# An expert layer's output side: gathering pv row by row, or streaming all of pv against a table of weights

## The reference

```python
def peer(h, w_pq, pk1, pk2, pu, pv):
    q = (h @ w_pq).reshape(n, P_HEADS, 2, P_HALF)
    s1 = jnp.einsum('nhd,hkd->nhk', q[:, :, 0], pk1)      # 128 keys each
    s2 = jnp.einsum('nhd,hkd->nhk', q[:, :, 1], pk2)
    v1, i1 = lax.top_k(s1, P_TOPK)                        # 16 best
    v2, i2 = lax.top_k(s2, P_TOPK)
    cand = (v1[..., :, None] + v2[..., None, :]).reshape(n, P_HEADS, P_TOPK * P_TOPK)
    cidx = (i1[..., :, None] * P_NKEYS + i2[..., None, :]).reshape(...)
    sc, j = lax.top_k(cand, P_TOPK)
    e = jnp.take_along_axis(cidx, j, axis=-1)             # 128 experts of 16384
    g = jax.nn.softmax(sc, axis=-1)
    a = jax.nn.gelu(jnp.einsum('nhkd,nd->nhk', pu[e], h), approximate=False)
    return jnp.einsum('nhk,nhkd->nd', g * a, pv[e])
h2 = layer_norm(DN_ALPHA * h1 + peer(h1, ...), ln2_g, ln2_b)
```

## Time and profile before

| what | us |
|---|---|
| runs (3) | 4841.81, 4850.69, 4885.9; median 4850.69 |
| span of the profiled execution | 4854.9 |
| busy PE, DVE, POOL, ACT | 3808.4, 2587.8, 2443.7, 821.8 |
| gathers L1351 and L1357, 1056 each | busy 1179.8 and 1225.1 |
| moved by the gathers' queue | 1107.96 MB |

### The profile page before, as it was taken

The page is one execution under the profiler, slowest core; times in us unless marked ns, Lnnn a source line. Parts: engine busy times, 40 slices in busy tenths (PEclk is TensorE's granted clock), DMA queues, the critical chain, the costliest instruction groups (busy, mean ns, idle before and its releaser), DMA issues.

```text
span 4854.9 us, 35025 instructions
## 1 busy us (share of the span) xinstructions
PE 3808.4 (78%) x10196; PEld 1735.7 (36%) x10196; DVE 2587.8 (53%) x5932; ACT 821.8 (17%) x1886; POOL 2443.7 (50%) x2256
## 2 busy tenths in 40 slices
PE   9899898878999667888676667677778667667677
PEld 4444445545664523333222222223234222222222
DVE  0323239997214675666565465465556656445453
ACT  1210123332100111111111111111111111111111
POOL 0000000000000077777777777777777777777776
PEclk9889989987799889999999999999999999999999
DMA  2100100000210499999999999999999999999998
GB/s 82 36 2 2 55 19 20 14 7 1 70 35 27 128 340 347 354 333 332 355 364 363 366 367 360 367 372 362 362 364 388 352 355 355 359 359 353 352 368 320
DMA packets 405562, 1185.00 MB, mean 244 GB/s; under 512 B 39936, under 2 KB 125248, under 8 KB 405264
## 3 DMA queue, kind: packets, MB, share of 16 engines
q0 software_dynamic: 304384, 1107.96, 61.2%
q1 hardware_dynamic: 101008, 74.99, 5.1%
HBM read 1176.60 MB, written 6.20 MB: 244 GB/s over the span
## 4 chain that ended last, share of the span: by engine, by line
POOL 20%; DMA 17%; PE 15%; issue 9%; DVE 5%; ACT 1%; POOLq 0%; DVEq 0%; SPq 0%; ACTq 0%
DMA v_rows<-in_pv,v_rows_at 14%; PE acc L1412 11%; POOL u_rows L1351 10%; POOL v_rows L1357 9%; PE pq_ps L1379 4%; DMA u_rows<-in_pu,u_rows_at 2%; DVE u_rows L1614 1%; PE key_ps L1387 0%; DVE key_at L1507 0%; DVE one_hot L1600 0%; ACT diag L1461 0%; DVE one_hot L1596 0%; DVE key_top L1504 0%; DVE top_at L1507 0%; DVE expert_f L1602 0%
## 5 line engine op out<-in xcount | busy, mean ns | idle before, releaser
L1412 PE MATMUL acc<-v_rows,diag 128*128 128x512 f32 (+1 forms) x4224 | 2064.5, 623 | 840.6 <-DMA v_rows<-in_pv,v_rows_at 587.5
L1614 DVE CUSTOM_DVE_ANT_0 u_rows<-u_rows,late 128x1024 f32<-128x1024 f32 x1056 | 1274.2, 1226 | 1061.5 <-DMA u_rows<-in_pu,u_rows_at 1054.7
L1412 PEld LDWEIGHTS acc<-v_rows,diag 128*128 128x128 f32 (+1 forms) x4224 | 751.2, 192 | 2135.1 <-issue 1261.4
L1357 POOL DMA_INDIRECT v_rows<-in_pv,v_rows_at x1056 | 1225.1, 1160 | 325.3 <-issue 235.8
L1351 POOL DMA_INDIRECT u_rows<-in_pu,u_rows_at x1056 | 1179.8, 1117 | 369.9 <-issue 291.3
L1461 ACT ACTIVATE diag<-ident_sb,expert_w 128x128 f32<-128x128 f32 x1024 | 379.7, 397 | 1451.4 <-PE acc L1412 1364.6
L1338 POOL COPY u_rows_at<-expert 128x16 uint32<-128x16 uint32 (+1 forms) x66 | 20.2, 306 | 1193.2 <-DVE expert L1605 1180.8
L1379 PE MATMUL pq_ps<-xT_sb,w_pq_sb 128*128 128x256 f32 (+2 forms) x768 | 238.8, 465 | 8.2 <-DMA iota_sb<-in_iota 7.6
L306 POOL DMA_DIRECT2D out_gla_p<-gla_S x4 | 2.3, 587 | 480.9 <-DVE gla_S L630 480.9
L1504 DVE MAX8 key_top<-key_scores 128x8 f32<-128x128 f32 (+1 forms) x288 | 68.1, 283 | 271.2 <-ACT key_scores L1447 171.3
L930 DVE MAX8 m<-score 128x8 f32<-128x384 f32 (+6 forms) x209 | 183.4, 878 | 5.3
(11 more groups left out here) (207 smaller groups left out, 3045.9 us busy)
## 6 DMA issues: line engine op xcount, KB each, us to landing
w_pq_sb<-in_w_pq SPq DMA_DIRECT2D x48, 512.0 KB, 12.6
u_rows<-in_pu,u_rows_at POOLq DMA_INDIRECT x1056, 6.2
v_rows<-in_pv,v_rows_at POOLq DMA_INDIRECT x1056, 6.2
xT_sb<-in_xT SPq DMA_DIRECT2D x8, 528.0 KB, 7.0
w_gvr<-in_w_in SPq DMA_DIRECT2D x2, 2048.0 KB, 13.0
w_gk<-in_w_in SPq DMA_DIRECT2D x8, 512.0 KB, 6.1
w_dsa<-in_w_in SPq DMA_DIRECT2D x2, 2048.0 KB, 10.3
w_b<-in_w_in SPq DMA_DIRECT2D x8, 512.0 KB, 4.2
```

The lines of the kernel that those rows point to most:

```text
L1357: pool.indirect_dma_start(out=V[:, j % RING, :], out_offset=None, in_=io["pv"], in_offset=bass.IndirectOffsetOnAxis(ap=atv[:, b, j:j + 1], ...
L1412: last = pe.matmul(acc[0:R, c * 512:(c + 1) * 512], dg[:, j % DG, 0:R], V[:, j % RING, c * 512:(c + 1) * 512], start=False, stop=False)
L1614: dve.tensor_tensor_reduce(U[:, j % RING, :], U[:, j % RING, :], h1[:, t, :], 1.0, 0.0, ALU.mult, ALU.add, dots[:, b, j:j + 1]).then_inc(d ...
```

## The change

pv is no longer gathered. `run_experts` is rewritten, and has these parts:
- `merge` also writes h1 to DRAM (`h1_d`), and `late` is given up ahead of `run_experts`. All keys' tops are found for the three groups; SP spills them to DRAM and POOL reloads them tile by tile.
- POOL gathers pu rows through one `ring` of 7 buffers, which also takes h1 tiles and the norm's gain and offset, in the order of the list `order`.
- The 8 tiles make 4 `PAIRS`. pv is cut into 128 blocks of 128 experts (512 KB, contiguous), which SP streams once for each pair through `pv_rows` (`NPV` = 4 buffers): 512 loads.
- A table holds, for a pair, the weight of each of 256 tokens for each of 16,384 experts. Expert number = 128 i1 + i2. For each token DVE writes two 128x128 marks (`marks`, `NOH` = 4 buffers): from i2, one where it equals the column; from i1, the weight where it equals the column. PE multiplies the two (`build`), which gives a 128x128 matrix: partition i2, column i1. ACT copies four of these at a time into the table (`move`), laid out as [partition i2, token, i1] in four pieces of 64 values of i1; the first piece lies in the memory of `xT_sb`, the others are called `table`. There is one table: `move` of a pair waits for the `product` before.
- `product`: for block i of pv, PE multiplies table[:, all 128 tokens, i], which is 128 columns in steps of 64 words, with the block's rows: four matmuls of 512 columns (2 tiles x 2 halves) into `acc` of 4 banks.
- DVE does the dots of the next pair (`products`) during `product`, with the picks of the tiles after between them. `take` and `norm` (the boundary's work) follow the next pair's marks. ACT stores y.
- The sample tile's pv rows are gathered still (32) and folded by DVE.

```diff
+    RING = 7
+    NPV = 4
+    NOH = 4
+    PAIRS = [(0, 1), (2, 3), (4, 5), (6, 7)]
...
+        order = rows(0) + rows(1) + rows(2) + rows(3) + after(0) + rows(4) + rows(5) + after(1) + rows(6) + rows(7) + after(2)
+        order += [("u", SAMPLE, j) for j in range(NS)] + [("v", SAMPLE, j) for j in range(NS)]
...
+                for n in range(len(PAIRS) * P):
+                    if n >= NPV:
+                        sp.wait_ge(pv_used, n - NPV + 1)
+                    e = (n % P) * P
+                    sp.dma_start(pvr[:, n % NPV, :], io["pv"][e:e + P, :]).then_inc(pv_in[n % NPV], 16)
...
+                        pe.matmul(tps[:, q % 2, (m % 4) * P:(m % 4 + 1) * P], onehot[:, m % NOH, 0, :], onehot[:, m % NOH, 1, :],
+                                  start=True, stop=True).then_inc(oh_used, 1)
...
+                        pe.wait_ge(pv_in[n % NPV], 16 * (n // NPV + 1))
+                        for x in range(2):
+                            for c in range(2):
+                                last = pe.matmul(acc[:, x, c * 512:(c + 1) * 512], table[x][i // 64][:, :, i % 64],
+                                                 pvr[:, n % NPV, c * 512:(c + 1) * 512], start=(i == 0), stop=(i == P - 1))
+                        last.then_inc(pv_used, 1)
...
+                    if x == 0 and t:
+                        act.wait_ge(pv_used, t // 2 * P)
+                    for q in range(P // 4):
+                        act.wait_ge(oh_used, t * P + 4 * q + 4)
+                        src = tps[:, q % 2, :].rearrange("p (n e) -> p n e", e=P)
+                        for y in range(2):
+                            last = act.copy(table[x][y][:, 4 * q:4 * q + 4, :], src[:, :, y * 64:(y + 1) * 64])
+                        last.then_inc(moved, 1)
...
+                        dve.tensor_scalar(onehot[:, m % NOH, 0, :], count[:], turned[:, t % 2, 1, n:n + 1], None, ALU.is_equal)
+                        dve.tensor_scalar(onehot[:, m % NOH, 1, :], count[:], turned[:, t % 2, 2, n:n + 1], turned[:, t % 2, 0, n:n + 1],
+                                          ALU.is_equal, ALU.mult).then_inc(oh_ready, 1)
...
+                first = [("keys", g, b) for g in (1, 2) for b in range(NB)] + pick(1)
+                products(0, HK, spaced(first, HK, HK))
+                products(1, HK, spaced(pick(2), HK, HK))
+                for p, pair in enumerate(PAIRS):
+                    if p:
+                        for t in PAIRS[p - 1]:
+                            take(t)
+                    for t in pair:
+                        prepare(t)
+                    for t in pair:
+                        marks(t)
+                    if p:
+                        norm(PAIRS[p - 1], p - 1)
+                    if p < 3:
+                        for t in PAIRS[p + 1]:
+                            products(t, HK, spaced(pick(t + 1), HK, HK))
```

More of the change, by code:

```diff
@@ L1179, in run_experts @@
-        st, mv = sb("ln2_st", [P, 12]), sb("ln2_mv", [P, 2])
[L1180 to L1185, removed]
@@ L1199, in group_tokens @@
+        place = {key: i for i, key in enumerate(order)}
         def group_tokens(g):
@@ L1201, in group_tokens @@
             return a, a + sum(ROWS[t] for t in GROUPS[g])
[L1207 to L1271, removed]
@@ L1301, in _ @@
[L1301 to L1314, removed]
-                for i in range(2 * NB + 2, 3 * NB):
-                    load(i)
@@ L1484, in _ @@
+                gelu(SAMPLE)
+                for t in (6, 7, SAMPLE):
+                    norm(t)
+                for t in (6, 7, SAMPLE):
+                    store(t)
+                act.wait_ge(y_out, 16 * TILES)
             @block.vector
@@ L1637, in _ @@
-                yl = Link(dve, y_step)
-                turns(dve, side, turn, boundary)
-                closers.pop(dve)
+                    link.add(ins)
+                    link.wait()
+                    for q in range(P // TS):
+                        dve.tensor_copy(weight[q * TS:(q + 1) * TS, t % 4, 0:NS], smp_w[:, q * NS:(q + 1) * NS])
+                        last = dve.tensor_copy(expert[q * TS:(q + 1) * TS, t % 4, 0:NS], smp_e[:, q * NS:(q + 1) * NS])
+                    last.then_inc(picked, 1)
@@ new lines, in landed, with products @@
+                def landed(key):
+                    i = place[key]
+                    dve.wait_ge(ring_in[i % RING], 16 * (i // RING + 1))
+                    return ring[:, i % RING, :]
+                def products(t, n, steps):
+                    dve.wait_ge(hd_in[t % 2], 16 * (t // 2 + 1) if t < SAMPLE else 16 * (t // 2) + 64)
+                    for k in range(n):
+                        u = landed(("u", t, k))
+                        dve.tensor_tensor_reduce(u, u, hd[:, t % 2, :], 1.0, 0.0, ALU.mult, ALU.add, dots[:, t % 2, k:k + 1]).then_inc(dot_done, 1)
+                        for s in steps[k]:
+                            side(*s)
@@ new lines, in _ @@
+                products(SAMPLE, NS, none)
+                w = weight[:, SAMPLE % 4, 0:NS]
+                dve.wait_ge(gelu_done, TILES)
+                link.wait()
+                link.add(dve.tensor_tensor(w, w, dots[:, 0, 0:NS], ALU.mult))
+                link.wait()
+                for j in range(NS):
+                    r = landed(("v", SAMPLE, j))
+                    if j == 0:
+                        dve.tensor_scalar(hd[:, 1, :], r, w[:, j:j + 1], None, ALU.mult).then_inc(v_done, 1)
+                    else:
+                        dve.wait_ge(v_done, j)
+                        dve.scalar_tensor_tensor(hd[:, 1, :], r, w[:, j:j + 1], hd[:, 1, :], ALU.mult, ALU.add).then_inc(v_done, 1)
@@ L1642, in streaming_step @@
+                dve.wait_ge(v_done, NS)
+                dve.sem_inc(fold_ready, 1)
+                for t in (6, 7, SAMPLE):
+                    take(t)
+                norm((6, 7, SAMPLE), 3)
 def streaming_step(nc, io):
```

571 lines of the change are left out of this document (330 added, 241 removed).

## The result

The changed kernel takes 4847.3 us (median of 19 runs), the kernel before 4885.2 beside it (19 runs): ratio 0.9947, 95% interval 0.9926 to 0.9968 (the two medians alone give 0.992). So the change gains a little, clear of the scatter, but less than the 1% that the prediction counts as a difference. The forecast was 2.7% slower than 4851, the median of the three runs at hand; against 4885 it would be 2.0%. The profiled span is 4845.5 us, 140 under the forecast's sum of 4986.

The account below looks back on a forecast made before the run. DMA at 364 GB/s was taken to bound the expert stage. Start and two tiles reach 2278 us; builds, takes and products 0 to 2 reach 4387, the last build 4516, last product 4960, tail 4986; predicted 4985, range 4790 to 5220.

Parts of the forecast that it names:

- The bound of the kernel before: Expert stage from about 1690 us: paid by the megabyte at 364 GB/s; 268 MB less would save 737 us.
- Products 0 to 2: First three pv products, beside the next pair's dots: DMA ends last, 565, 580 and 580 us.
- tiles and start: Stretches before the first build: first gather landed at 1723 us, then 340 and 215 us for two tiles.
- builds and end: Four table builds paced by DVE's marks, 126 and 3 x 129 us; closing stretches 444 and 26 us.
- Rival 4: pv streams: contiguous blocks make DMA faster, 388 GB/s, a product 34 us shorter, 4884 in all; chance 0.09 alone.
- Rival 3: pu gathers: dots hold POOL, 1.98 + 0.30 us on every gather, 5155 us in all; chance 0.11.
- tile 1: Second tile's pu gathers and dots, before the first build: POOL sets the pace, 215 us, bounds 189 and 293.
- Rival 2: Products' weight loads: the 64-word step sets the pace, 553 us a product, 5095 in all; chance 0.08.
- Rival 1: Builds: marks are faster than 0.47 us a token, at 0.29 the time is 4800 us; chance 0.17.
- Tile 0: First tile, before the first build: DVE's dots, remaining key tops and next pick take 340 us.
- the last product: Final pair's product: PE alone sets the pace, 444 us, against 277 us of data.
- the tail: After the final product: three takes, three norms, a store with its end and waits, 26 us.

Follow-up runs that it names:

- x5: Kernel before, with DVE's dot of a pu row with h1 replaced by a sum of the row; 4576.8 us, ratio 0.94.
- x10: Kernel before, with each tile's h1 copied by ACT to PSUM and the dots reading their second source there; 4568.7 us, ratio 0.9335.
- x1: Changed kernel, with each pv block's 128 rows lying 512 KB apart in DRAM instead of neighbours; ratio to the kernel before 0.9968.
- x2: Kernel before, with each pv gather taking 128 neighbouring rows instead of the picked ones; ratio 1.005.
- x4: Changed kernel, with each product's stationary operand read from neighbouring words instead of a step of 64; ratio to the kernel before 0.9972.
- x9: Changed kernel, with the first of a token's two marks written by POOL instead of DVE; 4983.5 us, ratio 1.0242.

## Why the prediction was wrong

**The bound of the kernel before** is the step that failed: "the stage is paid by the megabyte", with 364 GB/s as DMA's limit. A DMA share of 0.98 was taken for a full DMA, and the long gathers were set aside with "part of that is waiting". The share adds up the packets' durations: at 364 GB/s it read 0.98 with a mean of 174 ns, at 412 it reads 1.02 with 161. The median is 159 ns in both, and before 3.0% of the packets last over 300 ns, after 0.4%: long packets filled the share, not more bytes. The engine without rest was POOL, and that row stood in the earlier trace rows; only the 0.30 between its gathers was not added up. Runs x5 and x10 show it: with gathers of 0.95 us the same 1108 MB move at 404 and 403 GB/s.

**Products 0 to 2** carried that rate: 201.3 MB at 364 made 553, at 412 they make 489, and 507 to 536 came, since PE ends pv's part after 440 us and a remainder of pu goes on at 311 GB/s or less. That is 153 us less; all other terms together are 13 more, since tiles and start (40 more) and builds and end (27 less) happen to offset each other. And what the change takes off the bound of the kernel before is 1024 x 1.44 = 1475 us of POOL's time, not 737 us of transfers. The second and third product are 21 and 29 longer than the first, where 15 was put. The row of L1295 shows three waits of POOL on y's stores, 407 us together, most of it beside the builds; by the trace the first dot of these two products starts 11 us after the product's first matmul, and 1 us after it in the first. The rest of the 21 and 29 is not traced to a cause.

**Rival 4** (faster DMA) came nearest and for the wrong reason: 388 was no ceiling, and neighbouring rows do nothing (x1, x2). **Rival 3** was right in its mechanism, POOL held by the dots, but placed in the wrong kernel: it was the bound before, and after only that of tile 1 (235 for 215: 185.84 us of POOL and 134 gaps of 0.30 make 226) and of the products' ends. Nor does every gather take 1.98: in the kernel before those that start while a dot runs average 1.34, and the one at 4783.50 ends 0.81 us after the dot that ran as it started, not with a dot. **Rival 2** did not come: the load grew from 190 to 295 ns, where 433 were needed to set the pace. The Trainium skill ("Advanced Engine Details and Errata", "SBUF Cachelines") speaks of a penalty when each access takes a new line; x4 agrees in that the step costs 105 ns a load, all of it hidden. **Rival 1** came in small: marks every 0.45 us instead of 0.47, 116 for a build's 121.

Tile 0 was 12 longer, the last product and the tail as forecast. The serial structure stands as described: with transfers at 412 GB/s, the builds (491 us), two tiles without products (588) and a last product of PE alone (442) eat most of what leaving out 268 MB and 1024 gathers returns.

The Trainium skill, "SBUF — State Buffer", section "SBUF: two separate sides", calls the port pair that DVE and GpSimd share an exclusive lock: of a DVE operation with two SBUF inputs and a GpSimd operation that reads SBUF, the one that starts first has it for its whole length. The rows at 1.98 us and run x10 agree, if a gather counts as such an operation. The same section of the Trainium skill says that DMAs issued by GpSimd starve during DVE operations in a 2-port mode; here a dot with two sources does it. The Trainium skill's page "HBM Reference", "Specifications (TRN2)", gives about 425 GB/s to a core that streams alone; these runs show 412 to 418 while pv streams.

Not settled: why the rate in x5 and x10 stays at 404 and 403 GB/s where the changed kernel shows 412, and whether 412 to 418 is DMA's own limit or that of the seven ring buffers. No run changes their number.

## What to carry to other kernels

Before a rate is taken for a transfer limit, add the issuing engine's busy time and the gaps after its issues: if they fill the window, the rate may be the issuer's, and a run with shorter issues decides (x5, x10). A remedy that frees the issuer (here one operand of the dot in PSUM, -6.6%) can be worth far more than moving a quarter less. And a table that has to be complete before its first use makes a serial stretch: count what each engine does in it.

## What was not expected of the hardware

- A DVE dot with its second source in PSUM leaves POOL's gathers at 0.95 us (x10); with both in SBUF they average 1.12 to 1.16 in the kernel before, and single ones beside dots take 1.98.
- DMA share exceeds 1 (1.02 at 412 GB/s), and 0.98 at 364 GB/s was not a full DMA: x10 moves 403 through the same queue.
- A weight load of 128 fp32 columns with a step of 64 words takes 295 ns, of neighbours 190 (x4).
- A 128x128 compare with one scalar takes POOL 612 ns beside DVE's work (x9); on DVE its record reads 272 to 391 ns, and a pair of such marks goes by in 0.45 us whatever it reads.
